# Pairs of squared chunks added on VectorE ahead of TensorE's sums of squares, and the logarithm table loaded between the squares, in a two-layer hybrid transformer kernel

## The reference

```
def rms_norm(x, gain):
    xf = x.astype(jnp.float32)
    y = xf * lax.rsqrt(jnp.mean(xf * xf, axis=-1, keepdims=True) + EPS)
    return (y * gain.astype(jnp.float32)).astype(x.dtype)
...
    for l in range(DEPTH):
...
        h = modulate(rms_norm(x, norm_g[l, 0]), sh1, sc1)
        x = x + 0.5 * g1[:, None, :] * swiglu(h, w_ff_in[l, 0], w_ff_out[l, 0])
        h = modulate(rms_norm(x, norm_g[l, 1]), sh2, sc2)
        x = x + g2[:, None, :] * token_mix(h, ...)
        h = modulate(rms_norm(x, norm_g[l, 2]), sh3, sc3)
        x = x + 0.5 * g3[:, None, :] * swiglu(h, w_ff_in[l, 1], w_ff_out[l, 1])
```

## Time and profile before

| | |
|---|---|
| median of 3 runs | 1568.17 us (1568.08 to 1568.23) |
| the profiled execution's own time | 1571.36 us |
| its span | 1569.6 us |
| TensorE (PE) busy, weight loads (PEld) busy | 99%, 96% |
| VectorE (DVE) busy | 72% |
| ScalarE (ACT) busy | 51% |
| granted TensorE clock, mean | 0.997 |

### The profile page before, as it was taken

How to read it: one execution, slowest core, us unless ns; L and a number is a source line. 1 busy time by engine, 2 the same in 40 slices (tenths; PEclk the granted TensorE clock), 3 DMA queues, 4 the chain that set the end, 5 groups by cost and what they waited for, 6 DMA issues and landing times.

```text
span 1569.6 us, 29266 instructions
## 1 busy us (share of the span) xinstructions
PE 1548.2 (99%) x12591; PEld 1505.5 (96%) x12591; DVE 1133.6 (72%) x1533; ACT 801.0 (51%) x970; POOL 25.2 (2%) x29
## 2 busy tenths in 40 slices
PE   7999999999999999999999999999999999999998
PEld 6999999999999999999999999999999899999998
DVE  4597777898556988775877768769855588977444
ACT  2444336888446346433464333677855544453342
POOL 0000000000100000000000000000001000000000
PEclk9899999999999999999999999999999999999999
DMA  9879855554456885778558785554454589675451
GB/s 319 305 240 278 281 165 165 150 161 136 141 162 213 301 301 205 264 258 286 201 200 280 259 291 166 147 163 149 140 156 146 171 313 314 225 254 189 162 194 49
DMA packets 284001, 333.52 MB, mean 212 GB/s; under 512 B 13084, under 2 KB 235200, under 8 KB 283872
## 3 DMA queue, kind: packets, MB, share of 16 engines
q1 hardware_dynamic: 276112, 327.40, 63.0%
q10 hardware_dynamic: 7760, 4.26, 1.1%
HBM read 330.23 MB, written 1.38 MB: 211 GB/s over the span
## 4 chain that ended last, share of the span: by engine, by line
PE 86%; DVE 9%; ACT 2%; issue 1%; DMA 0%; SPq 0%; DVEq 0%; ACTq 0%
PE ps L490 73%; DVE w_lo L1438 3%; PE ps L837 3%; DVE scratch L1335 1%; PE ps L552 1%; ACT w_hi L964 1%; PE ps L752 1%; DVE hf L1482 1%; DVE h_lo L1487 1%; PE ps L620 1%; PE ps L553 1%; PE ps L698 1%; DVE xT L1502 1%; PE ps L799 1%; PE ps L514 1%
## 5 line engine op out<-in xcount | busy, mean ns | idle before, releaser
L490 PE MATMUL ps<-h_hi,w_hi 128*128 128x256 f32 x2336 | 666.1, 285 | 0.6 <-DVE w_lo L1438 0.6
L490 PE MATMUL ps<-h_lo,w_hi 128*128 128x256 f32 x2336 | 660.7, 283 | 0.0
L490 PE MATMUL ps<-h_hi,w_lo 128*128 128x256 f32 x2336 | 660.7, 283 | 0.0
L1438 DVE TENSOR_TENSOR w_lo<-raw,w_hi 128x2048 fp32r<-128x2048 f32 x237 | 541.4, 2286 | 124.9 <-ACT w_hi L964 124.9
L964 ACT ACTIVATE w_hi<-raw 128x2048 fp32r<-128x2048 f32 x237 | 452.1, 1910 | 207.0 <-PE ps L490 202.7
L490 PEld LDWEIGHTS ps<-h_hi,w_hi 128*128 128x128 f32 x2336 | 447.7, 192 | 8.7 <-issue 7.1
L490 PEld LDWEIGHTS ps<-h_lo,w_hi 128*128 128x128 f32 x2336 | 447.9, 192 | 0.5 <-issue 0.5
L490 PEld LDWEIGHTS ps<-h_hi,w_lo 128*128 128x128 f32 x2336 | 447.9, 192 | 0.0
L490 PE MATMUL ps<-xm_hi,w_hi 128*128 128x256 f32 x704 | 198.2, 282 | 0.0
L490 PE MATMUL ps<-xm_hi,w_lo 128*128 128x256 f32 x704 | 197.5, 281 | 0.0
L490 PE MATMUL ps<-xm_lo,w_hi 128*128 128x256 f32 x704 | 197.3, 280 | 0.0
(11 more groups left out here) (269 smaller groups left out, 1816.2 us busy)
## 6 DMA issues: line engine op xcount, KB each, us to landing
raw<-in_w_ff_in_dram SPq DMA_DIRECT2D x176, 512.0 KB, 4.7
eyr<-in_w_ada_dram SPq DMA_DIRECT2D x144, 512.0 KB, 6.9
raw<-in_w_in_dram SPq DMA_DIRECT2D x100, 512.0 KB, 4.7
raw<-in_w_ff_out_dram SPq DMA_DIRECT2D x88, 512.0 KB, 4.6
raw<-in_w_gate_dram SPq DMA_DIRECT2D x48, 512.0 KB, 4.6
raw<-in_w_branch_dram SPq DMA_DIRECT2D x48, 512.0 KB, 4.5
raw<-in_w_out_dram SPq DMA_DIRECT2D x16, 512.0 KB, 5.5
rgw<-in_rg_w_dram ACTq DMA_DIRECT2D x16, 128.0 KB, 2.2
```

Source lines behind the costliest of these rows:

```text
L490: last = mm(outs, a, b[:, cc, :], start=clear and cc == 0 and q == 0, stop=cc == n - 1 and q == 2, skip_group_check=True)
L1438: tt(w_lo[:, p % SPLIT, :], raw[:, p % RAW, :], w_hi[:, p % SPLIT, :].bitcast(F32), ALU.subtract).then_inc(lo_ready, 1)
```

## The change

Five times (at every norm but the first) VectorE adds the second squared chunk of each bank to the first, in place in `hf`, under a new semaphore `pair_ready`. TensorE waits for that instead of `sq_ready` and multiplies only the sum of the two by the matrix of ones: four float32 matmuls of 128 x 256 instead of eight. Inside a lead slab the sums move from behind its third chunk to behind its fifth. On ScalarE the table load moves from `norm`, behind all four banks' squares, to between banks 1 and 2.

```
@@ TensorE
                     for b in banks:
-                        pe.wait_ge(sq_ready, 4 * norm + b + 1)
-                        for cc in (2 * b, 2 * b + 1):
-                            last = mm(ps[:, 0, 0:T], ones[:, :], hf[:, cc, :], start=cc == 0, stop=cc == C - 1)
+                        pe.wait_ge(pair_ready, 4 * (norm - 1) + b + 1)
+                        last = mm(ps[:, 0, 0:T], ones[:, :], hf[:, 2 * b, :], start=b == 0, stop=b == 3)
...
-                        if cc == 2 and banks:
+                        if cc == 4 and banks:
                             sums(norm, *banks)
@@ ScalarE
                 def norm(q, p):
 
-                    ln_exp()
                     hi(p)
...
                             hi(up_in[0])
-                            expand(q, 0, 1, 2, 3)
+                            expand(q, 0, 1)
+                            ln_exp()
+                            expand(q, 2, 3)
                         else:
                             shift_column(3 * l + q)
                             hi(gate_in[0])
                             expand(q, 0, 1)
+                            ln_exp()
                             hi(up_in[0])
                             expand(q, 2, 3)
...
                 hi(k0 + K_GLR, cols=16)
-                expand(1, 0, 1, 2, 3)
+                expand(1, 0, 1)
+                ln_exp()
+                expand(1, 2, 3)
@@ VectorE
+                def square_pair(norm, b):
+
+                    dve.wait_ge(sq_ready, 4 * norm + b + 1)
+                    tt(hf[:, 2 * b, :], hf[:, 2 * b, :], hf[:, 2 * b + 1, :], ALU.add).then_inc(pair_ready, 1)
...
                         expand_low(following, 0, 1)
+                        square_pair(following, 0)
+                        square_pair(following, 1)
                         outputs_added(2)
                         outputs_added(3)
                         if e == 1:
                             lo(down[NF - 1] + 2)
+                        square_pair(following, 2)
+                        square_pair(following, 3)
                         expand_low(following, 2, 3)
...
                     if m == 3:
                         lo(k0 + K_OUT + 5)
+                    if m > 1:
+                        square_pair(3 * l + 2, m - 2)
                     residual(m, slab_done, k0 + K_OUT + m + 1)
                     if m > 1:
                         expand_low(3 * l + 2, m)
+                square_pair(3 * l + 2, 2)
+                square_pair(3 * l + 2, 3)
                 ff(1, 2)
```

More of the change, by code:

```diff
@@ L211, in build @@
         (slab_done, bank_done, hi_ready, lo_ready, ada_weighed, ada_done, ada_saved, act_steps, dve_steps, x_ready,
-         sq_ready, ss_done, rstd_ready, hf_ready, hhi_ready, h_ready, silu_ready, hid_made, hid_hi_ready, hid_ready,
+         sq_ready, pair_ready, ss_done, rstd_ready, hf_ready, hhi_ready, h_ready, silu_ready, hid_made, hid_hi_ready, hid_ready,
          consts_ready, bias_masked, fold_ready, ada_folded, ma_ready, mhi_ready, mlo_ready, xhi_ready, xlo_ready, lead_scaled, c_loaded, small_loaded, x_loaded, c_turned, turned, x_turned, par_ready, lam_ready, lam_exp,
@@ L222, in build @@
              "slab_done bank_done hi_ready lo_ready ada_weighed ada_done ada_saved act_steps dve_steps x_ready "
-             "sq_ready ss_done rstd_ready hf_ready hhi_ready h_ready silu_ready hid_made hid_hi_ready hid_ready "
+             "sq_ready pair_ready ss_done rstd_ready hf_ready hhi_ready h_ready silu_ready hid_made hid_hi_ready hid_ready "
              "consts_ready bias_masked fold_ready ada_folded ma_ready mhi_ready mlo_ready xhi_ready xlo_ready lead_scaled c_loaded small_loaded x_loaded c_turned turned x_turned par_ready lam_ready lam_exp "
```

## The result

The changed kernel takes 1601.09 us (median of four runs, 1597.52 to 1602.44) against 1568.12 beside it: a ratio of 1.0194, 95% interval 1.0182 to 1.0205, 33 us slower. The forecast was 1595.9 with a range of 1589 to 1604; rival B, with the clock falling twice at norms 2 and 5, stood at 1600.4.

What follows compares the result with a forecast made beforehand. TensorE, busy for 99% of the span, was taken to bound the kernel. Net +23.2 us at full clock plus 4.5 for the clock made 27.7 on the profiled 1571.36, or 1599.1; less the 3.2 offset, 1595.9 us, range 1589 to 1604.

Steps and rivals of the forecast that it cites:

- rival B: Clock falls again in the second wait of norms 2 and 5, or stays down longer: 4.5 more, 1600.4 us, chance 0.2.
- The saving, 8.6 us: TensorE at five norms: four fewer matmuls each, 20 x 0.43 = 8.6 us saved if nothing else moved.
- The addition, 0.40 us: VectorE: each addition of two squared chunks takes 0.40 us, with 0.33 before the next can start.
- Norms 1, 3 and 4: TensorE waits 2.0 us for bank 0's addition and saves 1.7; norm 3 waits 1.1 more: +0.3, +1.4, +0.3.
- Walked: Costs obtained by following the lists of TensorE, VectorE and ScalarE onward with the durations read from the profile.
- Norm 3's second wait: Additions push expand_low 2 behind what TensorE waits for at norm 3: a second wait of 1.1 us.
- Norms 2 and 5: Additions stand late in VectorE's list; TensorE waits 4.8, 5.6 and 3.5 us: 10.6 each, 21.2 for both.
- The table load, "costs nothing there": ScalarE at norm 1: the moved load falls in its 1.34 us wait for residual 2, so costs nothing there.
- full-clock sum: Net cost of all five norms with the clock staying up: 0.6 + 1.4 + 21.2 = +23.2 us.
- The clock, +4.5: TensorE's clock falls to half after the long waits of norms 2 and 5, losing 2.2 us each: +4.5.
- I take one such fall at each of norms 2 and 5: One clock fall at each; waits of 3.5 and 2.0 us left out as shorter than an earlier 4.6 us stretch.
- the offset that "the change does not touch": Whole kernel: the median of the runs lies 3.2 us below the profiled execution, taken as unaffected by the change.

Runs made afterwards that it cites:

- E11: E12 without the additions, so eight matmuls again, waiting for the squares: 1564.74 us against 1570.87 for the kernel before.
- E12: Changed kernel with all four sums in the first lead slab and VectorE's additions placed ahead of the second lead slab's lo: 1559.38 us against 1570.87 before.
- E3: Changed kernel with TensorE's waits for additions filled by matmuls of ones into an unused bank: 1590.94 us against 1570.62 for the kernel before.
- E4: Changed kernel with only VectorE's order at norms 2 and 5 changed, additions moved earlier: 1580.62 us against 1570.62 for the kernel before.
- E5: Changed kernel with only TensorE's list at norms 2 and 5 changed, sums of banks 0 and 1 behind product m = 3: 1586.32 us against 1570.88 before.
- E2: Kernel before the change with only the table load moved: 1568.54 us against 1570.62 for the kernel before, ratio 0.9989.
- E9: Changed kernel measured once more, beside E10 on the same chip: 1599.56 us, ratio 1.0192 to the kernel before.
- E10: E3's kernel with filled waits measured once more, beside the changed kernel: 1590.69 us, ratio 1.0130 to the kernel before.
- E1: Changed kernel with the table load back in its old place: 1602.82 us against 1570.62 for the kernel before, ratio 1.0207.

## Why the prediction was right, and where it was off

**The saving, 8.6 us.** Its matmuls are gone: 40 records where there were 80, and E11 against E12 shows their price at the seams, 1.6 to 1.7 us for four.

**The addition, 0.40 us.** It measured 0.42.

**Norms 1, 3 and 4.** Walked +0.3, +1.4, +0.3; in E3, where the clock plays no part, the table has +0.46, +0.94 and +0.20. The last two stretches begin with a feed-forward whose first slab is 0.71 and 0.27 us shorter, so the seams alone are +0.46, +1.65 and +0.47, 0.6 more than walked in all. The wait for bank 0 was 1.87 for 2.0. Norm 3's second wait shows as 0.3 us before `lead` in the changed kernel and 0.9 in E3, for 1.1 walked.

**Norms 2 and 5.** Walked 10.6 each at full clock; E3 has 10.66. The three waits were 4.68, 5.13 and 3.28 for 4.8, 5.6 and 3.5; the second is shorter in part because the sum before it, which met the fall of the clock, took longer. E4 and E5 show that it is the order of the two lists, since moving rows in either takes 13 to 19 us away.

**The table load, "costs nothing there".** True for the seam, but the sum has nothing for what comes behind. E2 shows that the load's place shortens it by 2.3 us, and the changed kernel's mixing blocks are likewise 0.5 us shorter each and its last feed-forward 0.7; in E3 these stretches and the two first slabs above give 2.8, of which no run attributes the 0.5 beyond E2. So the full-clock sum is not +23.2 but, by E3's marks without its start, +21.1.

**The clock, +4.5.** This is the term that was mis-sized: it measured 8.9 between the medians of E9 and E10, and 9.3 between the marks of the changed kernel and E3 (3.5 at each of norms 2 and 5, 1.5 at norm 1, 0.9 at norm 3). The price of the fall that was counted was about right: counted from the mark, the third sum of norm 2 comes 2.1 us later than in E3, for 2.2. The step that failed is "I take one such fall at each of norms 2 and 5", with the reason that waits shorter than the 4.6 us of the earlier trace rows would be spared. One row at the start of the program was too thin a ground for that: the clock was down again after the wait of 3.3 us, for 1.4 us at each of norms 2 and 5, and after 1.9 us at two of three norms, for 2.4 together.

The Trainium skill (TensorE: Matmul & The Clock Gate, "HAM oscillation — how this bites in real kernels") says that waits between bursts of matmuls make every burst begin at half clock. The traces agree for the bursts behind the second and third waits of norms 2 and 5, and disagree for the one behind 1.87 us at norm 4. The warning of the Trainium skill (same page, "Seeing it yourself") that clock events of a trace can be unreliable was not borne out here: in the dense rows of every stretch at 0.50, matmuls start 0.21 us apart.

Rival B's 1600.4 is nearer to 1601.09 than the forecast, but partly by luck: it puts 4.5 on the second falls of norms 2 and 5, which took 2.8, has nothing for norms 1 and 3, and shares the 2.1 too much of the full-clock sum.

**How the numbers close.** Between the two traces the forecast was +27.7 and the measured difference is +31.1: 2.1 less at full clock, 4.8 more for the clock (9.3 for 4.5) and 0.7 for a later start. About 1.9 us more of the 5.2 between 1595.9 and 1601.09 come from the offset that "the change does not touch": the profiled run of the kernel before lies 3.2 us above the median of its runs, that of the changed kernel 1.3 above its own. That the two mistaken terms go opposite ways helped the range hold.

## What to carry to other kernels

When work moves from a full engine to one with idle time, read where in the receiving engine's list it will stand and whether the full engine's queue stands still until then: at 71% busy, VectorE held TensorE up for 32 us before the sums, and with the same additions in other places of the two lists (E12) not at all there. Put a step whose input comes late behind work that does not need it, as here the sums inside a slab whose product needs no sum, and not ahead of such work, as the sums ahead of m = 3. And in this kernel a wait of TensorE has to be counted with a chance that the matmuls behind it run at half clock, even a wait of 2 us.

## What the runs showed that I had not expected

- Behind a wait of 1.87 us before a sum, in otherwise dense work, the granted clock went to 0.5 at norm 1 in one execution and left it at 1.00 in another of the same kernel, and at norm 4 in both. Five traces (the changed kernel, E1, E4, E5, E9) have this wait at each of norms 1, 3 and 4; the clock fell behind 9 of the 15. In E4 it also fell at norm 2 behind waits of only 1.4 and 0.6 us. What decides it no run shows.
- Filling the waits with 8 to 23 matmuls of ones by ones kept the clock at 1.00 and took 9 us off the changed kernel, for no useful work.
- The time of the program's start varies by up to 4 us between executions of any kernel here (first matmul on `h_hi` at 43.9 to 47.9 us).
- An earlier table load on ScalarE, off every chain that I had walked, was worth 2.3 us by the marks, in waits of 0.3 to 0.6 us for `w_lo` and `hid_lo` in the first 8 us behind the seams.
